# Shared expert's rows kept in SBUF, and the last LayerNorm's sums read by accumulating transfers

## The reference, cut to what matters

```
x   = LN(ALPHA*x + merged @ w_out)                 # 1088 x 1024
idx, w = route(x)                                  # top 8 of 64 experts, weights
shared = (silu(x @ w_sg) * (x @ w_su)) @ w_sd      # shared expert, hidden 256
y = 0;  y[toks] += (silu(xb @ wg[e]) * (xb @ wu[e])) @ wd[e] * w   # 64 experts, hidden 256
out = LN(ALPHA*x + y + shared)
```

## Time and profile before

| | us |
|---|---|
| median of 3 runs | 2419.66 (2417.68 to 2421.93) |
| the profiled execution | 2428.82 |
| its span, first to last instruction | 2426.9 |
| TensorE busy | 2284.9 (94%) |
| VectorE / ScalarE / POOL busy | 1405.8 / 963.1 / 1496.5 |
| DMA, mean over the span | 157 GB/s |

### The profile page before, as it was taken

How to read it: one execution, slowest core, us unless ns; L and a number is a source line. 1 busy time by engine, 2 the same in 40 slices (tenths; PEclk the granted TensorE clock), 3 DMA queues, 4 the chain that set the end, 5 groups by cost and what they waited for, 6 DMA issues and landing times. The chain is left out here.

```text
span 2426.9 us, 40519 instructions
## 1 busy us (share of the span) xinstructions
PE 2284.9 (94%) x15460; PEld 2011.2 (83%) x15460; DVE 1405.8 (58%) x2749; ACT 963.1 (40%) x1582; POOL 1496.5 (62%) x1525
## 2 busy tenths in 40 slices
PE   4999999999999999999998999999999999999882
PEld 4889899898898998989987776578898888888882
DVE  7365665755756647557567697534455555555344
ACT  3452734526436346263364232122323333333334
POOL 6355674675646646657467256577667777776533
PEclk9999999999999999999998999999999999999996
DMA  5201112011011111111112641599999999999995
GB/s 181 77 28 45 41 45 60 29 44 50 29 45 49 46 50 37 36 50 37 47 38 78 194 133 47 154 281 300 310 348 350 354 352 350 351 352 360 363 353 181
DMA packets 210602, 380.72 MB, mean 157 GB/s; under 512 B 25810, under 2 KB 132558, under 8 KB 209898
## 3 DMA queue, kind: packets, MB, share of 16 engines
q1 hardware_dynamic: 180218, 302.25, 34.8%
q0 software_dynamic: 30192, 75.89, 13.1%
HBM read 310.71 MB, written 76.41 MB: 160 GB/s over the span
## 5 line engine op out<-in xcount | busy, mean ns | idle before, releaser
L128 PE MATMUL ps<-xTh,w_mix_low 128*128 128x368 f32 (+1 forms) x1728 | 594.1, 344 | 7.0 <-POOL w_mix_low L122 5.7
L130 PE MATMUL ps<-xTh,w_mix_high 128*128 128x368 f32 (+3 forms) x1808 | 598.9, 331 | 0.4 <-issue 0.4
L129 PE MATMUL ps<-xTl,w_mix_high 128*128 128x368 f32 (+3 forms) x1808 | 597.1, 330 | 1.5 <-issue 1.5
L2298 POOL DMA_INDIRECT xg_early<-h_d,tabq_early x304 | 313.2, 1030 | 153.8 <-issue 80.8
L129 PEld LDWEIGHTS ps<-xTl,w_mix_high 128*128 128x128 f32 (+1 forms) x1808 | 340.1, 188 | 15.8 <-issue 9.5
L128 PEld LDWEIGHTS ps<-xTh,w_mix_low 128*128 128x128 f32 x1728 | 329.3, 191 | 20.5 <-issue 15.4
L130 PEld LDWEIGHTS ps<-xTh,w_mix_high 128*128 128x128 f32 (+1 forms) x1808 | 339.4, 188 | 5.6 <-issue 1.8
L2310 POOL DMA_INDIRECT ys_d<-yo,tab_early x114 | 216.6, 1900 | 112.6 <-issue 50.6
L122 POOL TENSOR_TENSOR w_mix_low<-w_mix_raw,w_mix_high 128x1024 fp32r<-128x1024 f32 x72 | 182.7, 2537 | 120.9 <-ACT w_mix_high L117 83.1
L1333 POOL TENSOR_TENSOR x_m<-x_m,kh_m 128x128 f32<-128x128 f32 (+1 forms) x272 | 125.4, 461 | 114.6 <-ACT x_m L866 114.6
L2340 PEld LDWEIGHTS ps<-xgT,wg_early 128*128 128x128 f32 x1376 | 177.6, 190 | 19.3 <-issue 18.6
(11 more groups left out here) (396 smaller groups left out, 4558.8 us busy)
## 6 DMA issues: line engine op xcount, KB each, us to landing
wd_early<-in_w_exp_down SPq DMA_DIRECT2D x43, 1024.0 KB
wg_early<-in_w_exp_gate SPq DMA_DIRECT2D x82, 512.0 KB
wu_early<-in_w_exp_up SPq DMA_DIRECT2D x82, 512.0 KB
w_mix_raw<-in_w_in SPq DMA_DIRECT2D x72, 512.0 KB, 3.8
wg<-in_w_exp_gate SPq DMA_DIRECT2D x42, 512.0 KB
wu<-in_w_exp_up SPq DMA_DIRECT2D x42, 512.0 KB
wd<-in_w_exp_down SPq DMA_DIRECT2D x21, 1024.0 KB
xg_early<-h_d,tabq_early POOLq DMA_INDIRECT x316
```

What stands on the lines that cost most here:

```text
L128: pe.matmul(out, ll, rh, start=start, stop=False)
L129: pe.matmul(out, lh, rl, start=False, stop=False)
L130: return pe.matmul(out, lh, rh, start=False, stop=stop)
L2298: pool.indirect_dma_start(out=xg[:, b, g, :], out_offset=None, in_=h2_d[:, :].rearrange("t (q n) -> (t q) n", q=4), in_offset=bass.Indirec ...
```

## The change

1. One SBUF buffer `shr` for all nine tiles of the shared expert's result (36 KB per partition) takes the place of the four buffers. Before its tiles are written it holds the shared expert's gate and up weights (tiles 2 to 5), the first LayerNorm's gain and bias (6, 7), and router weights, bias and small tables (8); `rows_out` waits for the last user of those.
2. `add_shared`, its waits and its semaphores are gone.
3. The last stage's reads are issued by POOL, not SP, and accumulate: `shr[t] += ys_d[t]`. The finished rows go to another buffer, `yn`.
4. The planes of expert 62 lie in the second buffers of the gate and up weights, those of expert 63 in `wdh`, `wdl`; both have a wait for the last reader.
5. Buffers are laid out anew for this; the path for overflowing experts (not taken with these inputs) clears `ys_d` first. `LATE` is renamed `BEHIND`.

```diff
 bridge():
-        gcol, bcol = sb("gcol1", [P, D]), sb("bcol1", [P, D])
+        shr = sb("shr", [P, NT, D])
+        wg, wu = (shr[:, t:t + 2, :]... for t in (2, 4))
+        gcol, bcol = shr[:, 6, :], shr[:, 7, :]
...
             def rows_out(t, b):
                 act.wait_ge(d_done, 2 * t + b + 1)
-                if b == 0 and t == 2:
-                    act.wait_ge(m_low, NT - 1)
-                if b == 0 and t >= 4:
-                    act.wait_ge(y_out[t % 4], 16 * (t // 4))
-                act.activation(shared_rows(t)[:m, cols(b)], ps[:m, (G, U)[b], :], ACT.Copy, scale=1.0 / ALPHA)...
+                if b == 0 and t == 6:
+                    act.wait_ge(y_ready, NT)
+                if b == 0 and t == 8:
+                    act.wait_ge(routed, NT)
+                act.activation(shr[:m, t, cols(b)], ps[:m, (G, U)[b], :], ACT.Copy, scale=1.0 / ALPHA)...
...
-            def add_shared(t):
-                m = rows(t)
-                pool.wait_ge(y_left, t + 1)
-                pool.wait_ge(y_right, t + 1)
-                pool.wait_ge(stored[t % 2], 32 * (t // 2 + 1))
-                pool.dma_start(ys_d[t * P:t * P + m, :], shared_rows(t)[:m, :], accum_op=ALU.add)...
...
             send(8)
-            add_shared(0)
-            add_shared(1)
-            add_shared(2)
-            add_shared(3)
-            add_shared(4)
             gather(0)
-            add_shared(5)
             gather(1)
-            add_shared(6)
-            add_shared(7)
-            add_shared(8)
 experts():
         def down_planes(e):
-            n = e - (NE - 2)
-            return (wdh[:, :, :], wdl[:, :, :]) if n < 0 else (last_planes[:, n, 0, :, :], last_planes[:, n, 1, :, :])
+            return (last_high[:, :, :], last_low[:, :, :]) if e == NE - 2 else (wdh[:, :, :], wdl[:, :, :])
...
             gather(2)
             pool.wait_ge(tab_s, 6)
-            for n in range(4):
-                pool.wait_ge(y_out[n], 16 * len(range(n, NT, 4)))
...
-                if e and e < NE - 2:
+                if e == NE - 2:
+                    act.wait_ge(u_done, e)
+                elif e == NE - 1:
+                    act.wait_ge(d_done, e - 1)
+                elif e:
                     act.wait_ge(d_done, e)
                 split_high(act, down_planes(e)[0], wds[e % DEEP]).then_inc(dh, 1)
 last_norm():
     def _(sp):
...
-        for rows_added, count in added:
-            sp.wait_ge(rows_added, count)
-        for t in range(NT):
-            m = rows(t)
-            sp.dma_start(xr[:m, t, :], ys_d[t * P:t * P + m, :]).then_inc(y_in[t], 16)
...
     def _(pool):
+        for rows_added, count in added:
+            pool.wait_ge(rows_added, count)
+        for t in range(NT):
+            m = rows(t)
+            pool.dma_start(xr[:m, t, :], ys_d[t * P:t * P + m, :], accum_op=ALU.add).then_inc(y_in[t], 16)
         pool.wait_ge(rows_in, 32)
```

More of the change, by code:

```diff
@@ L202, in build @@
             ns, nb, nl = (len(x.split()) for x in (SHARED_SEMAPHORES, BRIDGE_SEMAPHORES, LAST_SEMAPHORES))
-            bridge(nc, block, sems[:ns], sems[ns:ns + nb], a, ps, ident, ones, before, st, w_raw, w_high, late, woh, wol, mT_d, xn_d, h2_d, ys_d, tok_d, plan_d,
+            shr = bridge(nc, block, sems[:ns], sems[ns:ns + nb], a, ps, ident, ones, before, st, w_raw, w_high, late, woh, wol, mT_d, xn_d, h2_d, ys_d, tok_d, plan_d,
                    gates_d, only_d, dest_d, picks_d, pairs_d, step_d, limit_d, place, order, early)
@@ L206, in build @@
             c2 = ctx.enter_context(ExitStack())
-            first_experts(c2, "_reserved")
+            last_planes = []
+            for n in ("high", "low"):
+                c2.enter_context(nc.sbuf_tensor("first_of_two_" + n, [P, KT, FE], F32))
+                last_planes.append(c2.enter_context(nc.sbuf_tensor("last_" + n, [P, 2, D], F32R)))
+            first_experts(c2, "_reserved", 2)
             wg, wu, wd, xg, tab, tabw, tabq = early[:6] + early[-1:]
-            bufs = [wg, wu, wd, xg] + [c2.enter_context(nc.sbuf_tensor(n, shape, F32)) for n, shape in (
-                ("sl", [P, 2 * CAP]), ("yo", [P, 2, 2, D]))]
-            last, added = experts(nc, block, sems[:ns], sems[ns + nb:-nl], a, ps, ident, h2_d, ys_d, order, tab, tabw, tabq, bufs, c2)
+            bufs = [wg, wu, wd, xg]
+            last, added = experts(nc, block, sems[:ns], sems[ns + nb:-nl], a, ps, ident, h2_d, ys_d, order, tab, tabw, tabq, shr, last_planes, bufs, c2)
             last_norm(nc, block, sems[-nl:], a, o, ps, ys_d, added, *last)
@@ L1258, in _ @@
                 last_merge()
-                for k in range(EARLY, LATE):
+                for k in range(EARLY, BEHIND):
                     dve.wait_ge(wo_high, k + 1)
@@ L1910, in tables @@
                     dve.tensor_copy(tabw[:, some, j], ps[:, RB, n * NE:(n + 1) * NE][:, some]).then_inc(tab_s, 1)
-            for k in range(LATE, HEADS):
-                split_low(dve, wol[:, k, :], late[k - LATE], woh[:, k, :]).then_inc(wo_low, 1)
+            for k in range(BEHIND, HEADS):
+                split_low(dve, wol[:, k, :], late[k - BEHIND], woh[:, k, :]).then_inc(wo_low, 1)
             dve.wait_ge(first_high, 1)
@@ L2487 @@
                    "l_inverse l_gained l_ready l_offset l_unit l_scaled l_shifted l_stored")
+LAST_QUEUED = tuple(f"l_y{t}" for t in range(NT))
 BY_VECTOR = (1, 4, 7, 6)
@@ L2560, in scale_and_shift @@
             dve.wait_ge(gained, n + 1)
-            dve.scalar_tensor_tensor(out=xr[:m, t, :], in0=z[:m, n % 2, :], scalar=inverse[:m, t:t + 1], in1=shift[:m, :], op0=ALU.mult,
+            dve.scalar_tensor_tensor(out=yn[:m, t, :], in0=z[:m, n % 2, :], scalar=inverse[:m, t:t + 1], in1=shift[:m, :], op0=ALU.mult,
                                      op1=ALU.add).then_inc(y_ready, 1)
@@ L2670, in _ @@
                     sp.dma_start(dst, src).then_inc(lin, 16)
+                sp.wait_ge(blank, 1)
+                for t in range(NT):
+                    sp.dma_start(ys_d[t * P:t * P + rows(t), :], zero[:rows(t), :]).then_inc(wiped, 16)
+                sp.wait_ge(wiped, 16 * NT)
             @block.vector
@@ L2812, in _ @@
                                                      op1=ALU.add).then_inc(oy, 1)
-        with Phase(nc, LAST_SEMAPHORES) as (block, sems):
+        with Phase(nc, LAST_SEMAPHORES, LAST_QUEUED) as (block, sems):
             last_norm(nc, block, sems, a, o, ps, ys_d, (), *last)
```

93 lines of the change are left out of this document (49 added, 44 removed).

## The result

The changed kernel takes 2428.06 us (median of 6 runs, 2426.49 to 2429.24), the kernel before, beside it on the same chip, 2420.32 (6 runs, 2417.68 to 2422.39). The ratio is 1.0037 with a 95% interval of 1.0027 to 1.0047: slower by more than the 0.2% that a measurement can tell. The forecast was 2428.4.

What follows compares the result with a forecast made beforehand. TensorE was taken as busy for 94% of the span, with the weight stream last near the end. Terms -3.5 + 0 + 12.2 = +8.7 us on the median 2419.66 gave 2428.4 us, range 2415.5 to 2438.

Steps and rivals of the forecast that it cites:

- Part 1: Bridge's end: without the nine accumulating transfers and their waits the first expert starts 3.5 us earlier, carried to the end.
- The two new waits of `rows_out`: Bridge: they wait for work that ended 20 us before these copies, so cost 0.
- Rival C: Experts' queues: adds ahead of gathers and weights go, all 9 us come off, giving 2411 us; chance 0.08.
- Part 2: Last two experts' down planes in other buffers: the new waits are covered, cost 0.
- Part 3: Last stage: nine accumulating transfers at 2.56 us a tile land tile 7 later, so it ends 12.2 us later.
- Rival B: Last stage: accumulates cost twice only when writing to DRAM, onto SBUF run as plain reads; 2416.7 us; chance 0.14.
- rival D: Last stage: accumulated tiles land at 5.0 us each, net +28.5 us, giving 2448 us; chance 0.05.

Runs made afterwards that it cites:

- e1: The changed kernel with the last stage's nine transfers as plain reads issued by SP, leaving out the shared expert's rows; 2416.76 us.
- e2: The changed kernel with the last stage's nine transfers plain but still issued by POOL, leaving out the shared expert's rows; 2415.73 us.
- e3: The changed kernel with shared rows added onto DRAM behind the fourth and fifth gather, POOL waiting for them, and plain SP reads at the end; 2428.26 us.
- e7: The kernel before with only the down planes of the last two experts moved to dead buffers, with the new waits; 2419.02 us, ratio 1.0003.
- e6: The changed kernel with the last stage's nine transfers turned round, adding SBUF rows onto the DRAM sums; 2429.25 us, ratio 1.0047.
- e4: The changed kernel with shared rows added onto DRAM, tiles 0 to 3 before gather(0), 4 to 8 behind gather(2), and plain SP reads; 2419.11 us.
- e5: The changed kernel with the nine accumulating transfers issued in the order 1, 0, 4, 3, 7, 2, 6, 5, 8; 2424.03 us.

## Why the prediction was right

**Part 1, front: predicted -3.5, found.** The fronts of the profiles differ by 3.9 (31.4 against 35.3), after's by 3.2 from the first profile's (31.0, 34.2). The predicted start was 30.7 us behind the long row's start (1586.4 - 1555.73), measured 31.0. The gather was put too early by 1.3 us (5.11 to landing, 3.8 assumed from a plain load), so the transpose and not TensorE binds, by half a microsecond. By the runs the gain is 0.0008 (e1) and 0.0014 (e2), 1.9 and 3.4 us, with intervals that hold 3.5; e1's loses 2.9 us outside the span. That it is carried to the end shows in the table: the experts take 803.4 to 805.5 us in every kernel but e3, whether they start late or early, and the clock of the first matmuls accounts for a part of that spread. Rival C (9 us of backlog come off) is out by e1.

**The two new waits of `rows_out`: cost 0.** ScalarE's copies wait for TensorE alone in after. They were not taken out singly.

**Part 2: cost 0.** By e7's trace neither new wait is met; its runs say 0.0003, within 0.0012.

**Part 3, last stage: predicted +12.2, measured +13.3** in the tail (46.9 against 33.6). Tile 7 landed at S + 26.6 where 27.1 stood, the pass behind it took 13.23 as it should. The rest, 1.6 us (7.0 against 5.4 from the last scale to the span's end), I had not in the sum: it is the wait at line 102 (1.7 against 0.2), whose cause is open. The packet was put at 0.32 us and measured 0.295, so a tile is 2.4 us and not 2.56. With that the sum for tile 7 gives S + 25.5; the 1.1 us up to 26.6 I had not counted, and 0.6 of them are POOL's first issue, which starts that much after S. VectorE's waits inside its pass grew by 8.6 us, not by some 12, since part of the delay (17.9 against 14.8) lies ahead of its first tile. The mechanism stands by e2: without the accumulate the loss is gone. Rival B (twice as dear only when it writes to DRAM) is out by e6 and after, rival D (5.0 us a tile) by after.

**The sum.** +8.7 predicted; the medians differ by 7.7, the ratio of the runs says 9.0 (0.0037 x 2420), the stages of the profiles say 9.2. That 2428.4 meets the median to 0.4 us is luck: a packet put too dear, a first issue, a closing wait and 0.9 us outside the span that were not in the sum are each about 1 us and partly cancel. What was foreseen is the mechanism and its size. Adding the terms to the median rather than to the first profile's span mattered: by the spans the change would have looked 3 us faster.

**Left open:** what the DMA engines do while they count as full and move little behind a burst of accumulates with a gather after it (e4, 44 GB/s from 1566 to 1568; before has 64 GB/s at a share of 0.89 from 1574 to 1580); what held ScalarE in the first profile; what the wait at line 102 is, 1.7 us in after, e2, e5 and e6, 1.0 in e1 and 0.2 or 0.3 in the others; and what takes the time outside the span.

## What to carry to other kernels

An accumulating transfer cost the DMA engines 1.9 times a plain one here, in either direction, so it moves work rather than saving it: put it where transfers are hidden and no queue waits for it, not in a stage that only waits for DMA. In the order of use each accumulated tile of 512 KB in the last stage cost 0.9 us of the landing that decides. When a transfer becomes slow, look again at which tile decides and what stands behind it in each engine's order: the order of the transfers alone was worth 3 us. Compare kernels whose gain is a few microseconds by stages that begin and end at the same work, and with two profiles of the same kernel, before a span is believed.

## What the runs showed that I had not expected

- One execution of the kernel before ran 14 us late into the bridge's end, with ScalarE standing still without a known releaser; none of the eleven other profiles did.
- POOL issues plain 512 KB transfers that run at the same packet cost as SP's (0.155 and 0.153 us), and no loss from POOL's slower issue could be shown.
- Four accumulates ahead of a gather made its last transfer land in 9.77 us instead of 5.11.
- In five of twelve profiles the first expert's matmuls ran in part at half the clock and lost 1.5 to 3.0 us, in kernels with and without transfers in the bridge.
